# Turning the output rows of seven attention heads on VectorE instead of TensorE, in a two-block transformer kernel

## The reference, cut to what matters

```python
# block 1, retention, 4 heads of 256
scores = jnp.einsum('bhqd,bhkd->bhqk', qc, kc) * decay[None]
inner = jnp.einsum('bhqk,bhkd->bhqd', scores, vc)          # + cross and state over chunks of 128
o_ret = o_ret * lax.rsqrt(jnp.mean(o_ret * o_ret, axis=-1, keepdims=True) + EPS)
o_ret = o_ret.reshape(B, S, RET_WIDTH).astype(x.dtype) * ret_norm_w[l]
o_ret = jax.nn.silu(rg) * o_ret
merged = jax.nn.sigmoid(g_ret) * (o_ret @ w_ret_up[l]) + jax.nn.sigmoid(g_moba) * (o_moba @ w_moba_up[l])
# block 2, memory attention, 4 heads of 256
logits = jnp.einsum('bshd,bmhd->bhsm', q, k).astype(jnp.float32) * C_SCALE
p = jax.nn.softmax(logits, axis=-1).astype(v.dtype)
o_c = jnp.einsum('bhsm,bmhd->bshd', p, v)                   # then * silu(cz), @ w_branch[2]
```

## Time and profile before

| what | value |
|---|---|
| median of 3 runs | 2425.43 us (2425.33 to 2425.43) |
| the profiled execution | 2425.38 us, of which 2423.6 us are the span of the trace |
| PE busy in the span | 2416.7 us (100%) |
| DVE busy | 1738.4 us (72%) |
| ACT busy | 1238.4 us (51%) |
| POOL busy | 243.3 us (10%) |

### The profile page before, as it was taken

The page is one execution under the profiler, slowest core; times in us unless marked ns, Lnnn a source line. Parts: engine busy times, 40 slices in busy tenths (PEclk is TensorE's granted clock), DMA queues, the critical chain, the costliest instruction groups (busy, mean ns, idle before and its releaser), DMA issues.

```text
span 2423.6 us, 33998 instructions
## 1 busy us (share of the span) xinstructions
PE 2416.7 (100%) x10953; PEld 1994.0 (82%) x10953; DVE 1738.4 (72%) x2299; ACT 1238.4 (51%) x1612; POOL 243.3 (10%) x250
## 2 busy tenths in 40 slices
PE   9999999999999999999999999999999999999999
PEld 7888888878888888888888888888887888888887
DVE  5467677687877988988888887466667655587564
ACT  5445454555455444444444455455547555655443
POOL 0021243231000000000000000011101000521000
PEclk9999999999999999999999999999999999999999
DMA  7555555566655655555555556855554545555655
GB/s 271 191 190 173 179 179 182 203 214 226 209 194 174 203 191 193 191 195 191 187 193 199 194 190 211 251 186 175 173 186 161 179 160 182 177 169 166 225 183 165
DMA packets 134823, 464.21 MB, mean 192 GB/s; under 512 B 14544, under 2 KB 21328, under 8 KB 134112
## 3 DMA queue, kind: packets, MB, share of 16 engines
q1 hardware_dynamic: 122464, 443.08, 55.3%
q10 hardware_dynamic: 12256, 20.15, 2.6%
q0 software_dynamic: 32, 0.03, 0.0%
HBM read 455.87 MB, written 7.34 MB: 191 GB/s over the span
## 4 chain that ended last, share of the span: by engine, by line
PE 98%; DVE 1%; issue 0%; ACT 0%; DMA 0%; ACTq 0%; SPq 0%; DVEq 0%
PE PS L655 21%; PE PS L657 21%; PE PS L656 21%; PE PS L909 7%; PE PS L910 7%; PE PS L911 7%; PE PS L929 3%; PE PS L931 3%; PE PS L930 3%; PE PS L769 1%; PE PS L696 1%; PE PS L740 1%; PE PS L747 0%; DMA X<-x_in 0%; PE PS L777 0%
## 5 line engine op out<-in xcount | busy, mean ns | idle before, releaser
L1665 DVE TENSOR_TENSOR WL<-RAW,WH 128x1024 fp32r<-128x1024 f32 x842 | 1059.5, 1263 | 635.6 <-ACT WH L1137 626.5
L1137 ACT ACTIVATE WH<-RAW 128x1024 fp32r<-128x1024 f32 x841 | 889.3, 1060 | 1107.9 <-PE PS L657 725.8
L655 PE MATMUL PS<-WH,HT 128*128 128x512 f32 (+1 forms) x1816 | 717.9, 395 | 0.1
L657 PE MATMUL PS<-WH,HT 128*128 128x512 f32 (+1 forms) x1816 | 706.5, 389 | 0.0
L656 PE MATMUL PS<-WL,HT 128*128 128x512 f32 (+1 forms) x1816 | 705.5, 388 | 0.0
L655 PEld LDWEIGHTS PS<-WH,HT 128*128 128x128 f32 x1816 | 341.0, 188 | 73.0 <-issue 5.2
L657 PEld LDWEIGHTS PS<-WH,HT 128*128 128x128 f32 x1816 | 340.9, 188 | 71.1
L656 PEld LDWEIGHTS PS<-WL,HT 128*128 128x128 f32 x1816 | 341.3, 188 | 67.4
L909 PE MATMUL PS<-WH,HT 128*128 128x512 f32 x704 | 274.3, 390 | 0.0
L911 PE MATMUL PS<-WH,HT 128*128 128x512 f32 x704 | 273.9, 389 | 0.0
L910 PE MATMUL PS<-WL,HT 128*128 128x512 f32 x704 | 273.9, 389 | 0.0
(11 more groups left out here) (308 smaller groups left out, 2154.7 us busy)
## 6 DMA issues: line engine op xcount, KB each, us to landing
RAW<-w_stream SPq DMA_DIRECT2D x841, 512.0 KB, 3.3
bias_scratch<-BE ACTq DMA_DIRECT2D x12, 256.0 KB, 3.8
MEMR<-mem_in ACTq DMA_DIRECT2D x1, 2048.0 KB, 11.6
X<-x_in ACTq DMA_DIRECT2D x4, 512.0 KB, 4.2
x_scratch<-X ACTq DMA_DIRECT2D x4, 512.0 KB, 3.9
X<-x_scratch ACTq DMA_DIRECT2D x1, 2048.0 KB, 11.8
out<-X ACTq DMA_DIRECT2D x8, 256.0 KB, 3.3
X<-x_in SPq DMA_DIRECT2D x3, 512.0 KB, 9.2
```

Of the source, the lines that this page charges most:

```text
L655: pe.matmul(o, hi, WH[:, slot, kk, 0:cols], start=k == 0, stop=False)
L657: ins = pe.matmul(o, lo, WH[:, slot, kk, 0:cols], start=False, stop=k == nq * GK - 1)
L1137: act.activation(WH[:, g.slot(j)], RAW[:, g.slot(j)], ACT.Copy).then_inc(hi_split, 1)
L1665: dve.tensor_tensor(WL[:, s], RAW[:, s], WH[:, s].bitcast(F32), ALU.subtract).then_inc(lo_split, 1)
```

## The change

- OFT, 2 x 256 values on each partition, is new; it lies where the first block's VH was.
- For the RET heads and the C heads 0 to 2 (`rows_turned`), PE's four transposes of OF are gone. DVE turns OF into OFT itself in `rows_turn`: 8 transposes of 32 x 128 values in each of two steps, 8 and 9 for RET, 12 and 13 for C. Ahead of them it waits for its own o_rows and head_out; the last raises ot_done.
- ACT's and DVE's `head_output` read OFT instead of PSUM, one step later: 11 instead of 10 for RET, 15 instead of 14 for the three C heads.
- `head_values` waits for ot_done of the head before, since DVE itself now reads OF.
- The bias products stand one group later, at steps 3, 5, 8, 11, 13, 15; their one-hot matrices move with them.
- ACT's and DVE's loops over the C heads run three times, and the fourth head is written out behind them, with its output on PE as before.

```diff
+        OFT = sb("OFT", [P, 2, S], F32, at_u2 + 14 * KB)
...
+        def rows_turned(br, h):
+
+            return br is RET or br is CMEM and not isinstance(h, int)
...
-        BIAS_AT = (2, 4, 7, 10, 12, 15)
+        BIAS_AT = (3, 5, 8, 11, 13, 15)
...
-                st = head_steps(RET, H, lambda s: PA[:, s, ds(i * 256 + 2 * W, 256)], (None, 5, None, 7, 10))
+                st = head_steps(RET, H, lambda s: PA[:, s, ds(i * 256 + 2 * W, 256)], (None, 5, None, 7, None))
...
-                if p in st:
+                if p in st and not (p == 14 and rows_turned(CMEM, i)):
                     st[p]()
...
-                    ins = act.activation(dst, PS[:, bank:bank + 1, c * S:(c + 1) * S], ACT.Copy,
+                    src = OFT[:, c:c + 1] if rows_turned(br, h) else PS[:, bank:bank + 1, c * S:(c + 1) * S]
+                    ins = act.activation(dst, src, ACT.Copy,
...
-                elif p == 10:
+                elif p == 11:
                     head_output(RET, H, i)
...
-                st = head_steps(CMEM, At(C0, i, 1), At(8, i, 1), i, None, (None, 10, 11, 14))
+                st = head_steps(CMEM, At(C0, i, 1), At(8, i, 1), i, None, (None, 10, 11, 15 if rows_turned(CMEM, i) else 14))
...
                 dve.wait_ge(pv_done, H.count(1))
+                if dv > P:
+                    dve.wait_ge(ot_done, H.count())
...
+            def rows_turn(H, a0):
+
+                dve.wait_ge(o_rows, H.count(1))
+                dve.wait_ge(head_out, H.count(1))
+                for a in (a0, a0 + 1):
+                    for b in range(4):
+                        src = OF[32 * a:32 * a + 32].rearrange("p t (c d) -> p t c d", c=2)[:, :, :, 32 * b:32 * b + 32]
+                        dst = OFT[32 * b:32 * b + 32].rearrange("p c (t s) -> p t c s", t=T)[:, :, :, 32 * a:32 * a + 32]
+                        ins = dve.transpose(dst, src)
+                if a0:
+                    ins.then_inc(ot_done, 1)
...
-                    ps = PS[:, bank:bank + 1, c * S:(c + 1) * S]
+                    ps = OFT[:, c:c + 1] if rows_turned(br, h) else PS[:, bank:bank + 1, c * S:(c + 1) * S]
...
-                st = head_steps(RET, H, None, i, lambda t: PA[:, t, ds(i * 256 + 3 * W, 256)], (5, 8, 10))
+                st = head_steps(RET, H, None, i, lambda t: PA[:, t, ds(i * 256 + 3 * W, 256)], (5, 8, 11))
                 if p in st:
                     st[p]()
+                if p in (8, 9):
+                    rows_turn(H, 2 * p - 16)
...
+                    if turned and p in (12, 13):
+                        rows_turn(At(C0, i, 1), 2 * p - 24)
+            with dve.Fori(0, 3) as i:
+                ch.enter(i, 2)
+                c_block(i)
+            ch.leave(3)
+            c_block(3)
```

More of the change, by code:

```diff
@@ L1500, in c_step, with c_block @@
                     mem_gains(At(C0, i, 1))
-                st = head_steps(CMEM, At(C0, i, 1), At(8, i, 1), i, None, (None, 10, 11, 14))
+                st = head_steps(CMEM, At(C0, i, 1), At(8, i, 1), i, None, (None, 10, 11, 15 if rows_turned(CMEM, i) else 14))
                 if p in st:
                     st[p]()
-            with act.Fori(0, 4) as i:
-                ch.enter(i, 3)
+            def c_block(i):
                 g = At(GROUP0["a_proj"], i, 2 * GD)
@@ L1513, in _ @@
                     c_step(i, p)
-            ch.leave(4)
+            with act.Fori(0, 3) as i:
+                ch.enter(i, 3)
+                c_block(i)
+            ch.leave(3)
+            c_block(3)
             act.wait_ge(head_out, C0 + 4 + 1)
@@ L2100, in mem_turn, with c_block @@
                     ins.then_inc(qk_tr, 1)
-            with dve.Fori(0, 4) as i:
-                ch.enter(i, 2)
-                st = head_steps(CMEM, At(C0, i, 1), At(8, i, 1), i, lambda t: PB[:, t, ds(i * 256 + W, 256)], (9, 12, 14))
+            def c_block(i):
+                turned = rows_turned(CMEM, i)
+                st = head_steps(CMEM, At(C0, i, 1), At(8, i, 1), i, lambda t: PB[:, t, ds(i * 256 + W, 256)],
+                                (9, 12, 15 if turned else 14))
                 for p in range(2 * GD):
```

## The result

The changed kernel takes 2431.97 us in the median (2431.25 to 2433.34 in 9 runs), against 2425.43: the ratio is 1.0029, interval 1.0020 to 1.0038. That is 6.5 us slower, where 4.8 was forecast. The profiled execution took 2431.79 us, 2429.2 of them in the span.

A forecast was written before the change was run, and what follows sets the result against it. PE, busy for 2416.7 of 2423.6 us, was taken as the bound. RET transitions +6.7, fourth RET head -0.5, bias stage 0, C heads -1.5 gave +4.8 on 2425.38: 2430.2 us, range 2427.0 to 2433.8.

The forecast's parts named there:

- where DVE meets PE: Two places without slack: the RET scores, and the bias products, where five of twelve stall, 1.55 us in all.
- the one meeting of the earlier trace: RET scores: DVE's last turn ends at 381.80, PE's weight load starts at 381.95 and the scores at 382.01.
- PE's saving: Transposes taken off PE: 0.48 us per RET head, 0.49 per C head, 3.4 in all if nothing else moved.
- The turns' price: On DVE: eight transposes 2.51 to 2.53 us, 0.12 later start on another partition block, 0.16 wait ahead.
- the term, 2.08 for 2.24: RET heads 0 to 2: DVE's longer chain delays the next scores, 2.24 us net per transition, +6.7 for three.
- POOL beside the turns: RET heads: no collision between POOL and DVE's turns assumed; the other end was +0.6 us per head.
- Rival C: POOL and DVE also collide: +0.6 us for each of three heads, 0.8 at the first bias product; 2432.8; chance 0.16.
- What a wait on PE costs: RET scores: PE arrives 0.48 us earlier and waits 2.7; each transition costs 2.24 net.
- The bias stage: Bias products after the last RET head: stalls of 1.6 us against 1.55 before, so 0 (-1.2 to +1.2).
- the two ends given: First bias product's one-hot: ends at 484.3 if DI is done by 479.9, up to 486.0 if both collide.
- Rival B, the cover: RET turns cost PE nothing if rows_turn adds under 3.1 us to DVE's chain; 2422.0 or 2420.5; chance 0.12.
- The rule against the change: Turn 128x128 tiles on PE: 0.48 us there against 5.1 on DVE; a loss wherever DVE has no spare time.

The follow-up runs named there:

- c_only: The kernel before with only the first three C heads' output turned on DVE, RET heads and bias product steps as before: 2423.69 us.
- bias_only: The kernel before with only the bias products moved to steps 3, 5, 8, 11, 13, 15: 2423.65 us.
- late_scores: The changed kernel with RET's scores on PE and their decay on DVE in step 6 instead of 5: 2424.20 us.
- filled: The changed kernel with ten 512-column matmuls ahead of PE's wait for the last q/k turn in RET heads 1 to 3: 2430.25 us.
- fewer_turns: The changed kernel with 12 instead of 16 output turns for each RET head: 2425.32 us.
- late_mem: late_all with the 2 MB load, and ACT's wait for the last RET head ahead of it, moved between the two iterations of gates_ret: 2421.23 us.
- late_all: late_scores with the decay ahead of DVE's split in step 6 and the bias products at 4, 6, 8, 11, 13, 15: 2422.51 us.

## Why the prediction was right, point by point

- **What bounds the kernel, and where DVE meets PE.** Right. c_only gave what the sum had for it (-1.6 for -1.5), bias_only gave back all of the 1.55 us of stalls that the prediction had counted, and late_scores showed that the loss hangs on the one meeting of the earlier trace rows.
- **PE's saving, 0.48 us a head.** Right: the C stage gave 1.5 for three heads. (The rounded terms of the forecast's sum add up to 4.7; unrounded they give 4.77, the 4.8 of its last step.)
- **The turns' price.** Right: 2.51 and 2.52 us for eight, as in the earlier trace rows, and 1.26 us from split to turn on another partition block. The wait behind DVE's own rows was 0.04 us (360.19 + 0.86 = 361.05, to 361.09), not the 0.16 of the earlier trace rows; that is most of the error of the term, 2.08 for 2.24. The nearer row would have been one that waits on DVE's latest write alone.
- **POOL beside the turns.** I took no collision, and there was none: the turns from 361.09 to 363.60 kept 0.31 us each, and L530, beside them, took 0.74 us where the same operation beside a split (L525 before) took 1.73. The rule of the Trainium skill (GPSIMD Engine Reference, Specifications) that only DVE instructions with two SBUF inputs or in a 2-port mode contend agrees with that. Rival C fell with it, though the time came out near its number. L530 and the operation behind it:

```profile
361.05 0.74 POOL L530 TENSOR_TENSOR JK<-PA,CONST 128x256 f32<-128x256 f32 x1 [0.18 <-POOL QK L529]
361.97 0.74 POOL L531 TENSOR_TENSOR QK<-QK,JK 128x256 f32<-128x256 f32 x1 [0.18 <-POOL JK L530]
```

- **What a wait on PE costs.** This is the step that failed. The forecast had a wait cost its length. One of the three also took the clock down, and that cost 1.6 us more, a third of the forecast change; filled confirms it. Without it and the 0.8 outside the span the measured change would have been 4.0 against a forecast of 4.8: the terms that the sum had came out 0.8 too high together, and the two that it lacked added 2.4. So 6.5 for 4.8 is a sum of errors of both signs.
- **The bias stage.** 1.09 us at the first product, forecast 1.1; 0.3 at the second, forecast 0.34; none elsewhere. DI and the split of step 0 met in part: two splits in a row took 2.91 us there and 2.36 at 367.42. So the one-hot came about 0.55 us later than without a collision, between the two ends given.

```profile
487.62 2.91 DVE L1674 TENSOR_TENSOR WL<-RAW,WH 128x1024 fp32r<-128x1024 f32 x2 [0.68 <-ACT WH L1142]
```

- **Rival B, the cover.** Its point of decision can be read from fewer_turns: with 3.9 us of turns and wait added per head, the scores lie 36.66 and 36.64 us apart, 0.8 more than before (35.82 and 35.85). So the cover ends at 3.1 us, as the forecast had it.
- **The rule against the change** (VectorE: DVE Perf Modes, Rules for kernel authors, in the Trainium skill: 128x128 turns belong on TensorE where PSUM will do) came out right for the RET heads as they were placed, wrong for the C heads, where VectorE had spare time: -1.6 us. In late_mem, with the hand-overs moved, it was wrong for the RET heads too, by 0.5 us a head.

## What to carry to other kernels

When PE is busy all the time, an operation moved off it is worth its few tenths of a microsecond only if the other engine's chain has that much room up to the next hand-over to PE: read the start of the consumer against the end of the producer, and treat a hand-over with nothing to spare as a price of one for one. Where lateness moves from one hand-over to the next, as here from scores to decay, bias product and a bulk load, follow it to the end before giving up the move. And reckon that a PE wait of some two microseconds can cost the clock as well, as one of three did in the traces here.

## What the runs showed of the hardware that was not expected

- After PE had been idle for 2.35 us, and some 0.6 us after it had started again, the granted clock fell to its lower level (0.63, then 0.51 in 2 us stretches) for about 3.4 us, which cost 1.6 us; two other waits of 2.36 us in the same execution left it up, and three waits of 1.1 us in fewer_turns did too. Useless matmuls in the wait kept it up and made the kernel 1.7 us faster.
- In late_all, while a 2 MB load ran, ACT waited up to 3.6 us for a 512 KB weight group, and such groups took 6.1 us from issue to landing in the median; with the load moved away from there it was 3.6 us, and the waits were gone from that stretch.
- Kernels that differ only in DVE's and PE's instruction lists differ by 0.7 us in the time outside the span; the cause is open.
